# GpSimd makes the low part of every fourth piece of weights, in place of VectorE

## What is computed

```python
h = h + pool_mixer(rms_norm(h), pool_w) * pool_scale      # layer 0
h = h + squared_relu_mlp(rms_norm(h), w_mlp_in[0], w_mlp_out[0])
k, v = rms_norm(h) @ w_kv                                 # rotary on part of k
h = h + diff_attention(rms_norm(h), k, v, w_q, lam) @ w_o # layer 1
h = h + squared_relu_mlp(rms_norm(h), w_mlp_in[1], w_mlp_out[1])
return rms_norm(h, final_norm)
```

## Time and profile before

| | us |
|---|---|
| median of 3 runs | 1888.04 (1887.61 to 1889.03) |
| span of the profiled execution | 1886.5 |
| PE busy | 1851.7 |
| DVE busy | 1151.0 |
| ACT busy | 840.5 |
| POOL busy | 10.5 |

### The profile page before, as it was taken

One profiled execution on the slowest core, in us unless ns is written; L12 is line 12 of the kernel. 1 busy time (PEld: TensorE's weight loads), 2 busy tenths in 40 slices (PEclk: granted clock), 3 DMA queues, 4 the chain that ended last, 5 costly groups with the idle time before them and its releaser, 6 DMA issues.

```text
span 1886.5 us, 24435 instructions
## 1 busy us (share of the span) xinstructions
PE 1851.7 (98%) x8425; PEld 1539.2 (82%) x8425; DVE 1151.0 (61%) x1417; ACT 840.5 (45%) x1061; POOL 10.5 (1%) x14
## 2 busy tenths in 40 slices
PE   6999999999999999999999999999999999999997
PEld 5788888888888888888888888888888888888886
DVE  6755556665656565755556777565655565556665
ACT  5544444444444444744435545444444444444442
POOL 0000000000000000000000000000000000000000
PEclk9999999999999999999999999999999999999999
DMA  7555555556565655556654446556566555555552
GB/s 263 184 191 184 189 188 178 191 190 197 180 198 181 194 185 192 161 191 196 195 192 149 139 153 212 181 182 193 185 194 193 191 189 187 189 189 178 184 194 89
DMA packets 178009, 348.69 MB, mean 185 GB/s; under 512 B 10594, under 2 KB 10676, under 8 KB 177332
## 3 DMA queue, kind: packets, MB, share of 16 engines
q1 hardware_dynamic: 177408, 346.33, 57.2%
q10 hardware_dynamic: 564, 1.88, 0.3%
HBM read 346.07 MB, written 2.10 MB: 185 GB/s over the span
## 4 chain that ended last, share of the span: by engine, by line
PE 57%; issue 38%; DVE 3%; ACT 1%; DMA 1%; POOL 0%; SPq 0%; POOLq 0%; DVEq 0%
PE bank L908 18%; PE bank L906 18%; PE bank L907 18%; PE bank L924 2%; DVE w_lo L588 1%; DMA raw<-in_pool_w 1%; DVE h L636 0%; DVE a_lo L614 0%; PE bank L1045 0%; ACT w_hi L379 0%; DVE h L730 0%; DVE scratch L727 0%; DVE scratch L702 0%; DVE b_lo L608 0%; PE bank L1061 0%
## 5 line engine op out<-in xcount | busy, mean ns | idle before, releaser
L379 ACT ACTIVATE w_hi<-raw 128x1024 fp32r<-128x1024 f32 x648 | 677.5, 1061 | 809.7 <-PE bank L908 806.6
L588 DVE TENSOR_TENSOR w_lo<-raw,w_hi 128x1024 fp32r<-128x1024 f32 x648 | 774.2, 1220 | 317.0 <-ACT w_hi L379 312.7
L906 PE MATMUL bank<-w_hi,a_hi 128*128 128x512 f32 x1344 | 528.3, 393 | 0.0
L908 PE MATMUL bank<-w_hi,a_lo 128*128 128x512 f32 x1344 | 524.0, 390 | 0.0
L907 PE MATMUL bank<-w_lo,a_hi 128*128 128x512 f32 x1344 | 523.7, 390 | 0.0
L906 PE MATMUL bank<-w_hi,b_hi 128*128 128x512 f32 x1248 | 488.4, 391 | 0.7 <-issue 0.7
L908 PE MATMUL bank<-w_hi,b_lo 128*128 128x512 f32 x1248 | 485.9, 389 | 0.0
L907 PE MATMUL bank<-w_lo,b_hi 128*128 128x512 f32 x1248 | 485.8, 389 | 0.0
L636 DVE TENSOR_TENSOR h<-bank,h 128x512 f32<-128x512 f32 x288 | 185.5, 686 | 230.4 <-PE bank L908 230.4
L908 PEld LDWEIGHTS bank<-w_hi,a_lo 128*128 128x128 f32 x1344 | 252.6, 188 | 52.8
L907 PEld LDWEIGHTS bank<-w_lo,a_hi 128*128 128x128 f32 x1344 | 252.9, 188 | 51.1
(11 more groups left out here) (81 smaller groups left out, 349.9 us busy)
## 6 DMA issues: line engine op xcount, KB each, us to landing
raw<-in_w_mlp_in SPq DMA_DIRECT2D x256, 512.0 KB, 3.8
raw<-in_w_mlp_out SPq DMA_DIRECT2D x256, 512.0 KB, 4.9
raw<-in_w_kv SPq DMA_DIRECT2D x64, 512.0 KB, 4.1
raw<-in_w_q SPq DMA_DIRECT2D x32, 512.0 KB, 4.9
raw<-in_w_o SPq DMA_DIRECT2D x32, 512.0 KB, 4.2
raw<-in_pool_w SPq DMA_DIRECT2D x8, 512.0 KB, 9.1
h<-in_x SPq DMA_DIRECT2D x2, 1024.0 KB, 6.3
out<-scratch SPq DMA_DIRECT2D x3, 512.0 KB, 4.7
```

The lines of the kernel that those rows point to most:

```text
L379: nc.scalar.activation(w_hi[:, n], raw[:, n % RAW], ACT.Copy).then_inc(hi_ready, 1)
L588: nc.vector.tensor_tensor(w_lo[:, n], raw[:, n % RAW], w_hi[:, n].bitcast(F32), ALU.subtract).then_inc(lo_ready, 1)
L906: nc.tensor.matmul(banks[tb][:], hi[:, tok], w_hi[:, n, kk, :], start=begin, stop=False)
L908: last = nc.tensor.matmul(banks[tb][:], lo[:, tok], w_hi[:, n, kk, :], start=False, stop=end)
```

## The change

In every strip the low parts of pieces 3 and 7 (those in raw[3]) are made by GpSimd with the same subtraction. The one semaphore `lo_ready` becomes two, one for each engine; SP and PE wait for the one that belongs to the piece. GpSimd's small jobs are put between its pieces.

```diff
-        lo_ready = sem("lo_ready")
+        lo_dve = sem("lo_dve")
+        lo_pool = sem("lo_pool")
...
-                        sp.wait_ge(lo_ready, s * HALVES + n - RAW + 1)
+                        if n % RAW == RAW - 1:
+                            sp.wait_ge(lo_pool, s * 2 + n // RAW)
+                        else:
+                            sp.wait_ge(lo_dve, s * 6 + (n // RAW - 1) * 3 + n % RAW + 1)
...
-            for k in range(3):
-                inv_rms(k)
+            def low(s):
+
+                for n in (RAW - 1, 2 * RAW - 1):
+                    pool.wait_ge(hi_ready, s * HALVES + n + 1)
+                    nc.gpsimd.tensor_tensor(w_lo[:, n], raw[:, n % RAW], w_hi[:, n].bitcast(F32), ALU.subtract).then_inc(lo_pool, 1)
+
+            inv_rms(0)
+            low(0)
+            low(1)
+            inv_rms(1)
+            with nc.gpsimd.Fori(2, S_KV) as s:
+                low(s)
+            low(S_KV)
+            inv_rms(2)
+            with nc.gpsimd.Fori(S_KV + 1, S_Q + 3) as s:
+                low(s)
             for t in range(PAIRS):
+                low(S_Q + t + 3)
                 pool.wait_ge(o_mean_done, t + 1)
                 nc.gpsimd.tensor_tensor(o_rms[:, t, :], o_mean[:, t, :], neg_half[:], ALU.pow).then_inc(o_rms_done, 1)
-            for k in range(3, 5):
-                inv_rms(k)
+            low(S_Q + PAIRS + 3)
+            low(S_MLP[1])
+            inv_rms(3)
+            with nc.gpsimd.Fori(S_MLP[1] + 1, STRIPS) as s:
+                low(s)
+            inv_rms(4)
...
                 for n in (2 * g, 2 * g + 1):
+                    if n % RAW == RAW - 1:
+                        continue
                     dve.wait_ge(hi_ready, s * HALVES + n + 1)
-                    nc.vector.tensor_tensor(w_lo[:, n], raw[:, n % RAW], w_hi[:, n].bitcast(F32), ALU.subtract).then_inc(lo_ready, 1)
+                    nc.vector.tensor_tensor(w_lo[:, n], raw[:, n % RAW], w_hi[:, n].bitcast(F32), ALU.subtract).then_inc(lo_dve, 1)
...
-                    pe.wait_ge(lo_ready, s * HALVES + n + 1)
+                    if n % RAW == RAW - 1:
+                        pe.wait_ge(lo_pool, s * 2 + n // RAW + 1)
+                    else:
+                        pe.wait_ge(lo_dve, s * 6 + n // RAW * 3 + n % RAW + 1)
```

## The result

The changed kernel takes 1891.28 us (median of 18 runs, 1889.57 to 1892.56), the kernel before 1887.79 us (18 runs): a ratio of 1.0018, 95% interval 1.0011 to 1.0024, some 3.4 us slower. The profiled execution has a span of 1887.4 us. That is one of the shorter ones: the spans of this kernel's 18 runs fall in two groups, 1887.4 to 1887.7 (5 runs) and 1889.2 to 1889.6 (13 runs). Lines have moved: w_hi L379 is L402, w_lo on DVE L588 is L613, on POOL L369, the matmuls L906 to L908 are L934 to L936, `turn` L924 is L952, the transposes L1061 are L1089, L710 is L735, L730 is L755, L614 is L639, L834 is L859, L870 is L895, L874 is L899.

What follows compares the result with a forecast made beforehand. TensorE, busy 98% of the span, bounds the kernel; VectorE matters only where TensorE waits for it. Start +0.6 and attention +0.6 and +1.2 give +2.4 us on 1888.04: 1890.4 us, range 1882 to 1896.

Steps and rivals of the forecast that it cites:

- PE's turn, forecast near 55.2: In the start, TensorE's turn at 54.62 moves to 55.2; coming before 54 would show the prediction wrong.
- the group of 46.85: TensorE's matmul group in the start, waiting for VectorE's held residual add, would start near 48.55 instead of 46.85.
- The steady part costs nothing: Between start and attention, VectorE's relief only becomes idle time and even full exclusion fits: zero, beat still 44.41 us.
- The port: GpSimd's piece and VectorE's instructions with two SBUF inputs exclude each other; VectorE waits the whole 2.3 us at each meeting.
- rival 1: VectorE is not held by GpSimd, so its relief in start and attention wins 5.5 us: 1882.6 us; chance 0.23.
- GpSimd's piece, 2.3 us: Each 128x1024 subtraction on GpSimd takes 2.3 us, one pass for each input without overhead; 3.9 us carried to the range.
- Attention, +1.8: In attention, GpSimd's pieces delay VectorE in two rounds, costing TensorE 0.6 and 1.2 us; two other rounds zero.
- The start, +0.6: In the start, VectorE's relief against port holds leaves the low activations and TensorE's turn 0.6 us late.
- The meeting that I placed on the second block's addition: In the start, GpSimd's piece at 44.9 holds the residual add due at 45.0 until 47.2: loss 1.7 us.
- The clock: Eight matmuls behind the start's 2.05 us wait run at the lower clock level: 1.6 us, carried both ways.
- The loop bound at 4.7 us: Raw buffer 3's loop of high part, low part and landing binds only from a GpSimd piece of 4.7 us.
- Rival 2: GpSimd's piece is slow, 3.9 us, and holds the port in five meetings: +10.4 us, 1898.4 us; chance 0.26.

Runs made afterwards that it cites:

- the run with both places back on DVE: Changed kernel with GpSimd's pieces in the start and four in attention returned to VectorE, GpSimd keeping 154; against the kernel before: 1888.34 us, ratio 1.0003.
- The run without reads: Changed kernel with GpSimd's pieces replaced by a four-column subtraction and zero fills, part of the result left out; against the kernel before: 1882.02 us, ratio 0.9973.
- the all-DVE kernel: Changed kernel's two semaphores kept, but VectorE makes all low parts and GpSimd none; against the kernel before: 1888.05 us, ratio 1.0003.
- the repeat: The changed kernel, unaltered, timed and profiled once more against the kernel before: 1890.43 us, ratio 1.0017.
- the run with doubled pieces: Changed kernel with GpSimd making each of its pieces twice, one after the other; against the kernel before: 1915.13 us, ratio 1.0148.

## Why the prediction was right, step by step

Forecast +2.4 us, no measurable difference or slightly slower; measured +3.4 (2.1 to 4.5 by the interval). The prediction took 0.2% as the least that can be told from no change; the interval, 0.11 to 0.24%, is finer than that, and by it the changed kernel is slower. In attention the mechanism was right. In the start it was not, and one of the prediction's own signs of being wrong came true: PE's turn, forecast near 55.2, came at 53.09, ahead of the 54 that it named, and the group of 46.85 came 1.4 us earlier, not later. That the sum still fits is in part luck.

- *The steady part costs nothing.* Right: the beat is 44.42 us, and 154 pieces make no difference in the run with both places back on DVE.
- *The port.* The step taken on half a row held: DVE waits whole for GpSimd too. Shown by the lengths of L859 and L613. The run without reads points the same way: it came to 5.0 us below before, where rival 1, no holding, was worked out at 5.5 below.
- *GpSimd's piece, 2.3 us.* Measured 2.40 where it met nothing. One pass for each input at VectorE's pace was a guess that fitted; no run shows that this is how the time comes about.
- *Attention, +1.8.* Measured +1.91 in waits (0.28 + 1.08 + 2.27 - 1.72), and +2.1 in time from the fourth turn to the end. The split is different: I gave nothing to the first round, where the tiny `o_mean` was held, and 1.2 us to the last, where 0.55 was added, because PE itself came later by then. Taking the four pieces away gave back all that could be measured.
- *The start, +0.6.* The working failed, and whether the size fits is open. Against a profile of before's lower group (the all-DVE kernel, PE's fourth turn at 67.4 us) the two profiles of the change have the same turn at 68.0 and 68.8, +0.6 and +1.4; against the profile of before (69.2) they are 1.2 and 0.4 us earlier. By the measured +3.4 less 2.1 behind the start, the start costs about 1.3 us in the median, twice the forecast. The meeting that I placed on the second block's addition, by 0.1 us in a schedule carried, went the other way in both profiles; the third and fourth blocks were held instead. A schedule by hand can't decide an order by a tenth.
- *The clock.* Right to carry 1.6 us both ways: it is there in some executions of both kernels and absent in others. 13 of the 18 runs of the change lie in its upper group (spans 1889.2 to 1889.6), 4 of 11 in the repeat, 35 of 78 of the kernel before; that may be where the rest of 3.4 over 2.1 + 0.6 lies. No execution of the change's upper group was profiled, so it was not settled.
- *The loop bound at 4.7 us* was too low, a mis-sized term: I took a median landing of 5.0 us and 0.3 us of hand-overs on top, 6.4 us with the high part; what lies between GpSimd's pieces, load and high part together, took 5.1 to 5.9. The conclusion drawn from it, cost zero at 2.3 us, stands.

Rival 2, the slow piece, did not come, since a piece takes 2.40 us and not 3.9. What the run with doubled pieces lost, 28 us, shows how fast its price grows.

## What to carry to other kernels

Moving work off an engine that has idle time wins nothing in the steady state and can lose where that engine is late; list the few places where the bottleneck waits for it, and ask of each what the other engine will be doing just then. In this kernel GpSimd's subtractions did not run beside VectorE's two-input instructions: give GpSimd such pieces only where nothing urgent of VectorE's has to run within one of them (2.4 us here), two-input instructions above all. A change of order on the late engine can be worth more than its relief, if what is put off frees no buffer that others wait for.

## What the runs showed of the hardware that was not expected

- DVE's `o_mean`, a scalar operation on 128x4 elements with one input, took 1.63 us instead of 0.16 while GpSimd had the port (1029.84), and 1.24 us in the last round (1117.89). So not only two-input instructions are held. GpSimd's fills, which read nothing, held it as well: 0.55 us, up to the end of the fill at 1026.43. The Trainium skill (SBUF — State Buffer, section Who interferes with whom) has `tensor_scalar` among the operations that can enter a mode with both ports, and both rows agree; that it was in this mode no row shows.
- DVE is held inside its instruction, and the profile counts this as busy time: 733.6 us for 486 low parts, against 587.1 in the run where GpSimd fills.
- After the same idle of 2.05 to 2.07 us ahead of the second turn, PE's granted clock fell to its lower level in one profile (the kernel before) and stayed up in another with the same order of work (the all-DVE kernel). The runs of either kernel fall in two groups 1.6 us apart.
